# One quarter of the gate-weighted one-hots on GpSimd, and four moves around the first value tiles of an expert layer

## Chip, cores and metric

The kernel runs on one core of one Trainium2 chip. The metric is the device time of one execution in microseconds (us). The kernel before takes 2701.08 us (median of 3 runs, 2700.83 to 2701.56).

## What is computed

The reference is a network of two blocks on 256 tokens of width 1024. Nearly all the time of this case lies in two equal stages of the second block, one expert layer in each of its two layers:

```python
def peer(h, w_q, sub_keys, u_emb, v_emb):        # 8 heads, 128 keys a side, 16384 experts, top 16
    q = einsum('td,dhk->thk', x_t, w_q)
    s = einsum('thpk,hpnk->thpn', q, sub_keys)
    sv, si = lax.top_k(s, K)
    ...
    fv, fpos = lax.top_k(cand, K)
    eidx = take_along_axis(cidx, fpos, axis=-1)
    gate = softmax(fv, axis=-1)
    act = gelu(einsum('thkd,td->thk', u_emb[eidx], x_t))
    return einsum('thk,thkd->td', gate * act, v_emb[eidx])
```

## The kernel before

Nothing is gathered. The layer is computed densely: all 16384 experts are taken as 128 tiles of 128. For each tile TensorE makes the scores of 256 tokens (`u`, 128 x 1024), ScalarE applies Gelu, VectorE multiplies by a dense gate (zero where a token did not choose an expert), and TensorE adds the product with `v` (128 x 1024) onto four accumulator banks. To keep fp32 accuracy with the rounded `fp32r` type, an operand is split into a high part (a rounded copy) and a low part (the operand less its high part), and each product is three matmuls.

An expert layer `l` (0 or 1) runs in these stages, written out by hand for each engine and tied by semaphores:

1. Queries, keys and the top 16. TensorE, between other work, scores the first 14 tiles (`CHOICE_TILES`), kept in `early`.
2. The gate stage. Tokens are taken in 64 groups of four (`NG`, `GROUP`). For group `g` VectorE (`one_hots`) makes four plain one-hots in one instruction (L1517) and four gate-weighted ones in four (L1519), into one of two buffers `hot[:, g % 2]`; TensorE (`gate_products`, L714) multiplies them into one bank; ScalarE copies 114 of 128 tiles' gates from the bank to `gates` (L1010); VectorE (`gate_early`, L1529) multiplies the other 14 straight into `early`. Between two groups TensorE scores one or two of the eight slices of a further tile (`early_scores`, L689), 12 tiles over the stage (`GATE_TILES`), kept in `meanwhile` by ScalarE (L998).
3. The early values. The 26 tiles of `EARLY` already have scores, so only values are left, 12 matmuls a tile (L450). `VALUES` is their order: the 12 of `meanwhile` first, then the 14 of `early`. Per tile ScalarE makes the high part of `v` (L1019) and VectorE, in `early_expert`, makes the product with the gate (L1580, first 12 only), its high and low part (L1539, L1543), and the low part of `v` (`early_v_low`, L1543, 128x1024). Both are two tiles deep: ScalarE's high part of tile `n` waits for the values of `n - 2`. Also in this stage: the transposed input `HT` is split into parts (`split_ht_part`, from tile `SPLIT_AT` = 12 on), a diagonal for the second modulation gain is made (L1298) before tile `G2_AT` = 20 and multiplied after it (L754), and the last two tiles split the first `u` of the next stage.
4. The main loop over the other 102 tiles, scores and values, with TensorE without a pause. The change does not touch it.

SyncE issues all DMAs in one program order. `v` has three slots: the load of tile `n` waits for the low part of tile `n - 3` (`expert_v`), because the low part goes to another buffer and frees the slot. The three first `u` loads of the main loop stand together behind `v` tile 15 and wait for `early_read`, the sign that `meanwhile` has been read.

```python
for n in range(E_SLOTS, EARLY):
    fetch_v(n % E_SLOTS, v[VALUES[n]], split=base + n - E_SLOTS + 1)
    if n == GATE_TILES + E_SLOTS:
        sp.wait_ge(sem("early_read"), l + 1)
        for j in range(EARLY, EARLY + E_SLOTS):
            fetch_u(j % E_SLOTS, u[j])
```

Of the kernel before, what the change touches and what calls it, by code (L numbers as in the profile page):

```python
# [20 lines left out]
KT = D // P  # L21
T = 256
NB = T // P
# [32 lines left out]
P_SLOTS = 4  # L56
CHOICE_TILES, GATE_TILES = 14, 12
AFTER_CHOICE, AFTER_EXP = 12, 8
SPLIT_AT, G2_AT = 12, 20
EARLY = CHOICE_TILES + GATE_TILES  # L60
LATE = TILES - EARLY

# [35 lines left out]
    return [(CHOICE_TILES + n, [s % KT for s in every if s // KT == n]) for n in sorted({s // KT for s in every})]  # L98


VALUES = [*range(CHOICE_TILES, EARLY), *range(CHOICE_TILES), *range(EARLY, TILES)]


def program(nc, d, out):
    ctx = ExitStack()
    with ctx:
# [327 lines left out]
        def _(pe):  # L434
# [227 lines left out]
            def experts(l):  # L662
# [45 lines left out]
                def gate_products(g):  # L708
                    u = g % 2
                    pe.wait_ge(sem("hot"), l * NG + g + 1)  # L710
                    if g >= 2:
                        pe.wait_ge(sem("gates_kept"), l * NG + g - 1)
                    for t in range(GROUP):
                        mm = pe.matmul(ps[:, 6 + u, t * P:(t + 1) * P], hot[:, u, 1, t, :], hot[:, u, 0, t, :],  # L714
                                       start=True, stop=True)
                    mm.then_inc(sem("gates_made"), 1)
# [30 lines left out]

                base = l * TILES
                for n in range(EARLY - 1):
                    expert_values(n, base + n + 1, first=(n == 0), low=exp_uh[:, n % 2] if n < EARLY - 2 else None)  # L750
                    if n == G2_AT:
                        pe.wait_ge(sem("diag"), SPREADS[f"g2_{l}"] + 1)
                        for i in range(8):
                            mm = pe.matmul(ps[:, 6 + i // 4, i % 4 * P:(i % 4 + 1) * P], ones, g2_diag[:, i * P:(i + 1) * P], start=True, stop=True)  # L754
                        mm.then_inc(sem("g2_spread"), 1)
# [81 lines left out]
        def _(act):  # L837
# [147 lines left out]
            def experts(l):  # L985
                root(f"peer_{l}", f"mix_{l}")
                for i in range(4):
                    for j in range(2):
                        h = 2 * i + j
                        put(pq_t[:, 2 * h:2 * h + 2].rearrange("p a t -> p (a t)"), ((("pq", l, i), j), 0))  # L990
                        stored(f"pq_{l}_{h}")
                        put(sc[:, 2 * h:2 * h + 2].rearrange("p s b n -> p (s b n)"), (f"sc_{l}", h))
                        stored(f"sc_{l}_{h}")

                def keep_scores(n):
                    act.wait_ge(sem("expert_scored"), l * TILES + n + 1)
                    dst = early[:, n] if n < CHOICE_TILES else meanwhile[:, n - CHOICE_TILES]
                    act.activation(dst, ps[:, 4 + n % 2, 0:T], ACT.Gelu).then_inc(sem("early_kept"), 1)  # L998

                for n in range(AFTER_EXP):  # L1000
                    keep_scores(n)
                act.wait_ge(sem("gate_in"), l + 1)
                act.activation(chosen_h[:, 2], fin_v.rearrange("p (h b) k -> p h b k", b=NB), ACT.Exp).then_inc(sem("gate_exp"), 1)
                for n in range(AFTER_EXP, CHOICE_TILES):
                    keep_scores(n)
                act.wait_ge(sem("slots"), 2 * l + 2)

                for g in range(NG):
                    act.wait_ge(sem("gates_made"), l * NG + g + 1)
                    act.activation(gates[:, g * GROUP:(g + 1) * GROUP, :], r3(ps[:, 6 + g % 2, :], GROUP)[:, :, CHOICE_TILES:], ACT.Copy)\  # L1010
                       .then_inc(sem("gates_stored"), 1)
                    for n, steps in gate_steps(g):
                        if KT - 1 in steps:
                            keep_scores(n)
                for n in range(EARLY + 1):
                    act.wait_ge(sem(f"expert_v{n % E_SLOTS}_arrived"), 16 * (l * len(range(n % E_SLOTS, TILES, E_SLOTS)) + n // E_SLOTS + 1))
                    if n >= 2:
                        act.wait_ge(sem("expert_used"), l * (TILES + 1) + n)
                    act.activation(exp_vh[:, n % 2], exp_v[:, n % E_SLOTS], ACT.Copy).then_inc(sem("early_v_high"), 1)  # L1019
                    if n == G2_AT + 2:  # L1020
# [65 lines left out]
        def _(dve):  # L1086
# [328 lines left out]
            def experts(l):  # L1415
# [95 lines left out]
                def one_hots(g):  # L1511

                    u, at_ = g % 2, g * GROUP
                    if g >= 2:
                        dve.wait_ge(sem("gates_made"), l * NG + g - 1)
                    rows_of = slots_t[:, 0, at_:at_ + GROUP].unsqueeze(2).to_broadcast([P, GROUP, P])
                    dve.tensor_tensor(hot[:, u, 0], iota.unsqueeze(1).to_broadcast([P, GROUP, P]), rows_of, ALU.is_equal)  # L1517
                    for t in range(GROUP):
                        ins = dve.tensor_scalar(hot[:, u, 1, t, :], iota, slots_t[:, 1, at_ + t:at_ + t + 1],  # L1519
                                                slots_t[:, 2, at_ + t:at_ + t + 1], ALU.is_equal, ALU.mult)  # L1520
                    ins.then_inc(sem("hot"), 1)
# [9 lines left out]
                for g in range(NG):  # L1531
                    one_hots(g)
                    if g >= 2:
                        gate_early(g - 2)
                for g in (NG - 2, NG - 1):
                    gate_early(g)
                def high(dst, src):

                    return dve.tensor_copy(dst, src)  # L1539
# [18 lines left out]
                def early_v_low(n):  # L1558

                    v_arrived(n)  # L1560
                    dve.wait_ge(sem("early_v_high"), l * (EARLY + 1) + n + 1)
                    low(exp_uh[:, n % 2] if n < EARLY - 2 else exp_vl[:, n % E_SLOTS], exp_v[:, n % E_SLOTS], exp_vh[:, n % 2]).then_inc(sem("expert_v"), 1)

                def split_ht_part(k):

                    step(high(ht_high[:, k], HT[:, k]))
                    settle()
                    ins = low(ht_low[:, k], HT[:, k], ht_high[:, k])
                    if k == KT - 1:
                        step(ins)  # L1570
                        settle()
                        dve.sem_inc(sem("ht_split"), 1)
                    else:
                        step(ins)

                def early_expert(n):

                    dve.wait_ge(sem("expert_used"), base_v + max(n, 1))
                    if n < GATE_TILES:
                        step(dve.tensor_tensor(act_e[:, n % 2], meanwhile[:, n], gates[:, :, n], ALU.mult))  # L1580
                        x = act_e[:, n % 2]
                        settle()
                    else:
                        x = early[:, n - GATE_TILES]
                    step(high(act_h[:, n % 2], x))
                    u = n + 2
                    if u >= EARLY:
# [6 lines left out]
                    if n == GATE_TILES - 1:  # L1594
# [4 lines left out]
                    early_v_low(n)  # L1599
# [190 lines left out]
            end_rows("end2", HN)  # L1790


        @block.sync
        def _(sp):
            sp.dma_start(X.rearrange("p b n -> p (b n)"), d["x"]).then_inc(sem("x_loaded"), 16)
# [12 lines left out]
            def load_experts(l):  # L1808
# [24 lines left out]

                chunk_read(1)
                chunk_read(2)
                for n in range(P_SLOTS // 2):
                    fetch_early(n)
                chunk_read(3)
# [4 lines left out]
                for n in range(P_SLOTS, EARLY):  # L1843
                    fetch_early(n)
                for n in range(E_SLOTS, EARLY):
                    fetch_v(n % E_SLOTS, v[VALUES[n]], split=base + n - E_SLOTS + 1)
                    if n == GATE_TILES + E_SLOTS:
                        sp.wait_ge(sem("early_read"), l + 1)
                        for j in range(EARLY, EARLY + E_SLOTS):
                            fetch_u(j % E_SLOTS, u[j])  # L1850
                turns = LATE // STEP - 1
                for n in range(EARLY, EARLY + STEP):
                    if n >= EARLY + E_SLOTS:
# [164 lines left out]
```

## Time and profile before

| | us |
|---|---|
| median of 3 runs | 2701.08 (2700.83 to 2701.56) |
| the profiled execution | 2696.82, its span 2694.8 |
| TensorE matmul busy | 2483.4 (92% of the span) |
| VectorE busy | 1916.7 (71%) |
| ScalarE busy | 427.9 (16%) |
| GpSimd busy | 0.2, in four 128x1 memsets |
| gate stage, layer 0 | first group's products at 790.6, last scores end near 904.7 |
| early values, layer 0 | 908.05 to 985 |

How to read it: an engine's busy time is an average over stages with different limits. For each of the stages named above one looks at which engine runs back to back, and at what the others' idle time is put down to. Matmul records have modelled ends, so distances between starts are the safer durations. `x8` of an fp32 matmul is four matmuls of two passes each.

### The profile page before, as it was taken

The numbers are of one execution on the slowest core, as the hardware profiler recorded it, in microseconds if no ns is written. First come the engines' busy times: TensorE is split into PE (matmuls) and PEld (weight loads), VectorE is DVE, ScalarE is ACT, GpSimd is POOL, SyncE is SP. The second block draws the span as 40 slices with busy tenths as digits, with TensorE's granted clock in tenths as the row PEclk, the third lists the DMA queues.
The fourth block names the chain that finished last, engine by engine and source line by source line (L and its number), as shares of the span: only waits on it lengthen the run. The fifth ranks groups of instructions, "written<-read, shape, count | busy, mean of one in ns | idle before, by whom it ended". The sixth has DMA issues, their size and how long they took to land.

```text
span 2694.8 us, 37151 instructions
## 1 busy us (share of the span) xinstructions
PE 2483.4 (92%) x13514; PEld 2071.3 (77%) x13514; DVE 1916.7 (71%) x4362; ACT 427.9 (16%) x865; POOL 0.2 (0%) x4
## 2 busy tenths in 40 slices
PE   8987999887899999999999976689999999999997
PEld 6655787454787789999999955558777899999997
DVE  2324344453889878888888854559898888888887
ACT  2322000011123320000000023411233100000001
POOL 0000000000000000000000000000000000000000
PEclk9988999988999999999999988899999999999998
DMA  5413677733141255555555543023205455555553
GB/s 194 156 63 125 239 282 290 291 146 150 65 139 56 91 184 187 186 186 187 187 186 187 186 181 125 1 94 118 79 32 195 163 187 186 187 186 187 187 187 120
DMA packets 87211, 429.43 MB, mean 159 GB/s; under 512 B 10064, under 2 KB 10704, under 8 KB 77008
## 3 DMA queue, kind: packets, MB, share of 16 engines
q1 hardware_dynamic: 87120, 428.23, 45.0%
q8 instruction: 56, 0.92, 0.1%
q14 instruction: 35, 0.29, 0.0%
HBM read 427.14 MB, written 1.05 MB: 159 GB/s over the span
## 4 chain that ended last, share of the span: by engine, by line
PE 77%; DVE 16%; DMA 3%; ACT 2%; issue 2%; DVEq 0%; SPq 0%; ACTq 0%; PEldq 0%
PE ps L450 48%; PE ps L482 10%; PE ps L472 6%; DVE HN L1519 5%; PE ps L689 4%; DVE HN L1517 3%; PE ps L648 3%; DMA ring<-in_stream 2%; DVE arena L1271 1%; PE ps L512 1%; PE ps L530 1%; DVE HT L1151 1%; DVE arena L1529 1%; PE ps L676 1%; ACT arena L901 1%
## 5 line engine op out<-in xcount | busy, mean ns | idle before, releaser
L450 PE MATMUL ps<-ring_rounded,HN_rounded 128*128 128x512 f32 x3072 | 745.5, 393 | 11.5 <-DVE ring_rounded L1543 11.1
L450 PEld LDWEIGHTS ps<-ring_rounded,HN_rounded 128*128 128x128 f32 x3072 | 563.2, 189 | 130.5 <-issue 21.1
L450 PE MATMUL ps<-ring_rounded 128*128 128x256 f32 x3264 | 619.2, 283 | 0.0
L1543 DVE TENSOR_TENSOR ring_rounded<-ring,ring_rounded 128x1024 fp32r<-128x1024 f32 x460 | 561.9, 1222 | 16.7 <-ACT ring_rounded L1019 9.7
L450 PEld LDWEIGHTS ps<-ring_rounded 128*128 128x128 f32 x3264 | 522.3, 191 | 7.9
L450 PE MATMUL ps<-HT_rounded,ring_rounded 128*128 128x256 f32 x1632 | 461.8, 283 | 0.0
L1539 DVE CAST ring_rounded<-ring 128x1024 fp32r<-128x1024 f32 x406 | 280.5, 691 | 155.7 <-DMA ring<-in_experts_u 153.6
L482 PE MATMUL ps<-HT,ring 128*128 128x256 f32 x1472 | 335.7, 389 | 20.2 <-DVEq L1158 19.3
L482 PEld LDWEIGHTS ps<-HT,ring 128*128 128x128 f32 x1472 | 285.6, 196 | 62.4 <-DVEq L1158 21.1
L450 PEld LDWEIGHTS ps<-HT_rounded,ring_rounded 128*128 128x128 f32 x1632 | 312.5, 191 | 8.0
L1026 ACT ACTIVATE HN<-ps 128x256 f32<-128x256 f32 x204 | 78.3, 384 | 1061.6 <-PE ps L450 1061.6
L689 PE MATMUL ps<-HT,ring 128*128 128x256 f32 x832 | 201.8, 380 | 4.1 <-issue 1.5
L871 ACT ACTIVATE arena<-ps 128x512 f32<-128x512 f32 (+4 forms) x136 | 77.6, 581 | 557.2 <-PE ps L482 362.1
L689 PEld LDWEIGHTS ps<-HT,ring 128*128 128x128 f32 x832 | 148.0, 191 | 19.5 <-issue 3.1
L472 PE MATMUL ps<-ring,HT 128*128 128x512 f32 (+3 forms) x384 | 157.7, 572 | 5.1 <-DVEq L1158 5.1
L714 PEld LDWEIGHTS ps<-HN 128*128 128x128 f32 x1024 | 124.2, 191 | 47.4 <-DVE HN L1519 37.3
L714 PE MATMUL ps<-HN 128*128 128x128 f32 x1024 | 141.6, 281 | 13.8 <-DVE arena L1529 13.8
L1519 DVE TENSOR_SCALAR HN<-iota,slots_t 128x128 f32<-128x128 f32 x512 | 146.4, 375 | 0.0
L472 PEld LDWEIGHTS ps<-ring,HT 128*128 128x128 f32 x384 | 75.3, 198 | 83.1 <-issue 75.0
L1622 DVE TENSOR_TENSOR HN<-HN,arena 128x256 f32<-128x256 f32 x204 | 130.3, 639 | 10.9 <-ACT HN L1026 6.4
L1271 DVE SCALAR_TENSOR_TENSOR arena<-ring,cact,arena 128x256 f32<-128x256 f32 x336 | 135.0, 478 | 0.0
L1517 DVE TENSOR_TENSOR HN<-iota,slots_t 128x512 f32<-128x512 f32 x128 | 92.0, 719 | 9.9 <-PE ps L714 9.6
(204 smaller groups left out, 1746.7 us busy)
## 6 DMA issues: line engine op xcount, KB each, us to landing
ring<-in_stream SPq DMA_DIRECT2D x69, 2048.0 KB, 8.4
ring<-in_experts_u SPq DMA_DIRECT2D x256, 512.0 KB, 4.3
ring<-in_experts_v SPq DMA_DIRECT2D x256, 512.0 KB, 3.5
ring<-in_stream SPq DMA_DIRECT2D x2, 1024.0 KB, 7.6
arena<-in_keys SPq DMA_DIRECT2D x2, 1024.0 KB, 14.8
ring<-in_stream SPq DMA_DIRECT2D x1, 1664.0 KB, 8.3
ring<-in_stream SPq DMA_DIRECT2D x1, 1040.0 KB, 19.4
X<-in_x SPq DMA_DIRECT2D x1, 1024.0 KB, 4.9
```

What stands on the lines that cost most here:

```text
L450: mm = pe.matmul(out_, p, q, start=(first and i == 0), stop=(last and i == 2))
L472: mm = pe.matmul(t[:, 0:n], src[:, k, b * P:(b + 1) * P], w[:, k, :], start=(k == 0), stop=(k == nk - 1))
L482: mm = pe.matmul(t[:, j * T:(j + 1) * T], w[:, k, i * 256 + j * P:i * 256 + (j + 1) * P], src[:, k, :], start=(k == 0), stop=(k == KT - 1))
L648: mm = pe.matmul(down[2 * b + half], act_t[:, kt, b * P:(b + 1) * P], w[:, k, half * 512:(half + 1) * 512], start=(kt == 0), stop=(kt == F ...
L689: mm = pe.matmul(ps[:, 4 + n % 2, 0:T], pre_u[:, n % P_SLOTS, k * P:(k + 1) * P], HT[:, k, :], start=(k == 0), stop=(k == KT - 1))
L714: mm = pe.matmul(ps[:, 6 + u, t * P:(t + 1) * P], hot[:, u, 1, t, :], hot[:, u, 0, t, :], start=True, stop=True)
L1271: ins = dve.scalar_tensor_tensor(out=part, in0=wk, scalar=cact[:, k:k + 1], in1=part, op0=ALU.mult, op1=ALU.add)
L1517: dve.tensor_tensor(hot[:, u, 0], iota.unsqueeze(1).to_broadcast([P, GROUP, P]), rows_of, ALU.is_equal)
L1519: ins = dve.tensor_scalar(hot[:, u, 1, t, :], iota, slots_t[:, 1, at_ + t:at_ + t + 1], slots_t[:, 2, at_ + t:at_ + t + 1], ALU.is_equal, ...
L1539: return dve.tensor_copy(dst, src)
L1543: return dve.tensor_tensor(dst, src, h.bitcast(F32), ALU.subtract)
L1622: dve.tensor_tensor(act_e[:, j % 2], act_e[:, j % 2], g, ALU.mult).then_inc(sem("split_steps"), 1)
```

## The change

- `one_hots` makes three of the four weighted one-hots of a group; GpSimd makes the fourth, as one TENSOR_SCALAR of the same shape on the same operands, and signals `hot_last`. TensorE waits for it too. GpSimd waits, as VectorE does, until the products of group `g - 2` are made.
- `FIRST = 2`: the order of early values becomes two tiles of `early`, the 12 of `meanwhile`, the 12 other tiles of `early`.
- The first `v` tile: ScalarE makes its high part in the gate stage at group 58, VectorE its low part at group 61, in place, over the loaded tile. So the load into its slot (tile 3) waits for the values of tile 0 and no longer for its low part.
- The `u` loads stand behind `v` tiles 17, 19 and 21, one each.
- ScalarE makes the high parts of `HT` (tiles 14 to 21); VectorE keeps the low parts. The diagonal is made before tile 24 and multiplied after it.

```diff
-SPLIT_AT, G2_AT = 12, 20
+FIRST, SPLIT_AT, G2_AT = 2, 14, 24
-VALUES = [*range(CHOICE_TILES, EARLY), *range(CHOICE_TILES), *range(EARLY, TILES)]
+VALUES = [*range(FIRST), *range(CHOICE_TILES, EARLY), *range(FIRST, CHOICE_TILES), *range(EARLY, TILES)]
+def low_in_place(n):
+    return n == 0 or n >= EARLY - 2
...
                     pe.wait_ge(sem("hot"), l * NG + g + 1)
+                    pe.wait_ge(sem("hot_last"), l * NG + g + 1)
...
+                    if g == NG - 6:
+                        act.wait_ge(sem("expert_v0_arrived"), 16 * (l * len(range(0, TILES, E_SLOTS)) + 1))
+                        act.activation(exp_vh[:, 0], exp_v[:, 0], ACT.Copy).then_inc(sem("early_v_high"), 1)
-                for n in range(EARLY + 1):
+                for n in range(1, EARLY + 1):
...
+                    if SPLIT_AT <= n < SPLIT_AT + KT:
+                        k = n - SPLIT_AT
+                        act.activation(ht_high[:, k], HT[:, k], ACT.Copy).then_inc(sem("ht_high"), 1)
...
-                    for t in range(GROUP):
+                    for t in range(GROUP - 1):
                         ins = dve.tensor_scalar(hot[:, u, 1, t, :], iota, slots_t[:, 1, at_ + t:at_ + t + 1],
                                                 slots_t[:, 2, at_ + t:at_ + t + 1], ALU.is_equal, ALU.mult)
...
-                    step(high(ht_high[:, k], HT[:, k]))
-                    settle()
+                    dve.wait_ge(sem("ht_high"), l * KT + k + 1)
                     ins = low(ht_low[:, k], HT[:, k], ht_high[:, k])
...
+                    if n:
+                        early_v_low(n)
+                for g in range(NG):
+                    one_hots(g)
+                    if g >= 2:
+                        gate_early(g - 2)
+                    if g == NG - 3:
+                        early_v_low(0)
...
+        @block.gpsimd
+        def _(pool):
+            for l in range(2):
+                pool.wait_ge(sem("slots"), NB * (l + 1))
+                for g in range(NG):
+                    if g >= 2:
+                        pool.wait_ge(sem("gates_made"), l * NG + g - 1)
+                    t = g * GROUP + GROUP - 1
+                    pool.tensor_scalar(hot[:, g % 2, 1, GROUP - 1, :], iota, slots_t[:, 1, t:t + 1], slots_t[:, 2, t:t + 1],
+                                       ALU.is_equal, ALU.mult).then_inc(sem("hot_last"), 1)
...
+                U_AT = [FIRST + GATE_TILES + E_SLOTS + i for i in (0, 2, 4)]
...
+                    if low_in_place(n - E_SLOTS):
+                        fetch_v(n % E_SLOTS, v[VALUES[n]], base_v + n - E_SLOTS + 2)
+                    else:
+                        fetch_v(n % E_SLOTS, v[VALUES[n]], split=base + n - E_SLOTS + 1)
+                    if n in U_AT:
+                        j = EARLY + U_AT.index(n)
                         sp.wait_ge(sem("early_read"), l + 1)
-                        for j in range(EARLY, EARLY + E_SLOTS):
-                            fetch_u(j % E_SLOTS, u[j])
+                        fetch_u(j % E_SLOTS, u[j])
```

VectorE's queue over the end of the gate stage and the first two early tiles, layer 0, before (HN is where `hot` and the activation's parts lie, ring where `u` and `v` lie):

```order
L1529 TENSOR_TENSOR arena<-ps,arena 128x4x14 [waits gates_stored]
L1517 TENSOR_TENSOR HN<-iota,slots_t 128x512 [waits gates_made]
L1519 TENSOR_SCALAR HN<-iota,slots_t 128x128 x4
L1529 TENSOR_TENSOR arena<-ps,arena 128x4x14 [waits gates_stored] x3
L1580 TENSOR_TENSOR HN<-ring,arena 128x256 [waits gates_stored,expert_used,early_kept,dve_steps]
L1539 CAST HN_rounded<-HN 128x256 [waits dve_steps]
L1543 TENSOR_TENSOR HN_rounded<-HN,HN_rounded 128x256 [waits dve_steps]
L1543 TENSOR_TENSOR ring_rounded<-ring,ring_rounded 128x1024 [waits early_v_high,expert_v0_arrived]
```

The same place now:

```order
L1543 TENSOR_TENSOR arena<-ps,arena 128x4x14 [waits gates_stored]
L1551 TENSOR_TENSOR ring_rounded<-ring,ring_rounded 128x1024 [waits early_v_high,expert_v0_arrived]
L1531 TENSOR_TENSOR HN<-iota,slots_t 128x512 [waits gates_made]
L1533 TENSOR_SCALAR HN<-iota,slots_t 128x128 x3
L1543 TENSOR_TENSOR arena<-ps,arena 128x4x14 [waits gates_stored]
L1531 TENSOR_TENSOR HN<-iota,slots_t 128x512 [waits gates_made]
L1533 TENSOR_SCALAR HN<-iota,slots_t 128x128 x3
L1543 TENSOR_TENSOR arena<-ps,arena 128x4x14 [waits gates_stored] x3
L1547 CAST HN_rounded<-arena 128x256 [waits gates_stored,expert_used,early_kept,dve_steps]
L1551 TENSOR_TENSOR HN_rounded<-arena,HN_rounded 128x256 [waits dve_steps]
```

A group has three weighted one-hots instead of four, the low part of the first `v` tile stands two groups before the end, and only a cast and a subtraction of 128x256 are left between the gate stage and the first value matmul.

SyncE's queue over the early values, layer 0, before:

```order
L1816 DMA ring<-in_experts_u 128x1024 [waits expert_scored] x22
L1828 DMA ring<-in_experts_v 128x1024 [waits expert_v] x13
L1821 DMA ring<-in_experts_u 128x1024 [waits early_read]
L1821 DMA ring<-in_experts_u 128x1024 x2
L1828 DMA ring<-in_experts_v 128x1024 [waits expert_v] x11
```

And now:

```order
L1844 DMA ring<-in_experts_u 128x1024 [waits expert_scored] x22
L1856 DMA ring<-in_experts_v 128x1024 [waits expert_used]
L1856 DMA ring<-in_experts_v 128x1024 [waits expert_v] x14
L1849 DMA ring<-in_experts_u 128x1024 [waits early_read]
L1856 DMA ring<-in_experts_v 128x1024 [waits expert_v] x2
L1849 DMA ring<-in_experts_u 128x1024 [waits early_read]
L1856 DMA ring<-in_experts_v 128x1024 [waits expert_v] x2
L1849 DMA ring<-in_experts_u 128x1024 [waits early_read]
```

The first `v` load of the stage now waits for finished values, and the three `u` loads no longer stand in a row.

## Rows read from the trace of the kernel before

**Rows 1.** The page: span, and busy time of each engine with its share.
```profile
span 2694.8 us, 37151 instructions
PE 2483.4 (92%) x13514; PEld 2071.3 (77%) x13514; DVE 1916.7 (71%) x4362; ACT 427.9 (16%) x865; POOL 0.2 (0%) x4
```

**Rows 2.** Timeline (start us, us, engine, line, operation), VectorE, one group of gate stage 0.
```profile
841.55 0.28 DVE L1529 TENSOR_TENSOR arena<-ps,arena 128x56 f32<-128x56 f32 x1
841.71 0.72 DVE L1517 TENSOR_TENSOR HN<-iota,slots_t 128x512 f32<-128x512 f32 x1
842.31 1.14 DVE L1519 TENSOR_SCALAR HN<-iota,slots_t 128x128 f32<-128x128 f32 x4
843.34 0.29 DVE L1529 TENSOR_TENSOR arena<-ps,arena 128x56 f32<-128x56 f32 x1
```

**Rows 3.** Timeline, TensorE, the same stretch; in brackets idle time and who ended it.
```profile
840.24 1.08 PE L714 MATMUL ps<-HN 128*128 128x128 f32 x8
841.16 0.60 PE L689 MATMUL ps<-HT,ring 128*128 128x256 f32 x2
841.98 1.13 PE L714 MATMUL ps<-HN 128*128 128x128 f32 x8 [0.22 <-DVE arena L1529]
842.95 1.03 PE L689 MATMUL ps<-HT,ring 128*128 128x256 f32 x4
843.81 0.31 PE L714 MATMUL ps<-HN 128*128 128x128 f32 x1
```

**Rows 4.** Groups by form over gate stage 0 (busy us, mean ns | idle before).
```profile
L1519 DVE TENSOR_SCALAR HN<-iota,slots_t 128x128 f32<-128x128 f32 x256 | 73.2, 376 | 0.0
```

**Rows 5.** Chain of waits from the gate stage into the early values, layer 0.
```profile
905.34 0.65 DVE HN L1580
906.01 0.30 DVE HN_rounded L1539
...
906.69 1.23 DVE ring_rounded L1543
...
908.05 1.05 PE ps L450 x2
```

**Rows 6.** Windows around that passage (busy by engine, PEclk, DMA share, GB/s).
```profile
904.00:908.00 4.00, 0.70 (x4) 0.27 (x2) 2.84 (x6) 2.70 (x4) 0.00 (x0) 1.00 0.00 0
908.00:912.00 4.00, 3.95 (x10) 3.12 (x11) 2.31 (x4) 0.00 (x0) 0.00 (x0) 0.57 0.53 158
```

**Rows 7.** Timeline, TensorE, after each pause of the early values, layers 0 and 1.
```profile
956.22 11.36 PE L450 MATMUL ps<-ring_rounded,HN_rounded 128*128 128x512 f32 x48 [0.85 <-DVE ring_rounded L1543]
968.37 2.97 PE L450 MATMUL ps<-ring_rounded,HN_rounded 128*128 128x512 f32 x12 [0.80 <-DVE ring_rounded L1543]
982.28 2.98 PE L450 MATMUL ps<-ring_rounded,HN_rounded 128*128 128x512 f32 x12 [0.77 <-DVE ring_rounded L1543]
2071.65 11.39 PE L450 MATMUL ps<-ring_rounded,HN_rounded 128*128 128x512 f32 x48 [0.47 <-DVE ring_rounded L1543]
```

**Rows 8.** Timeline, TensorE elsewhere: the same 16 transposes after two idle times.
```profile
1701.44 2.05 PE L530 MATMUL ps<-arena 128*128 128x128 f32 x16 [1.52 <-ACTq L909]
243.69 3.78 PE L530 MATMUL ps<-arena 128*128 128x128 f32 x16 [2.36 <-ACTq L909]
```

**Rows 9.** Groups over the early values, layer 0, 905 to 985 us.
```profile
L1539 DVE CAST ring_rounded<-HT 128x256 fp32r<-128x256 f32 x8 | 2.3, 287 | 0.0
L1539 DVE CAST ring_rounded<-ring 128x1024 fp32r<-128x1024 f32 x2 | 1.4, 688 | 0.0
L1019 ACT ACTIVATE ring_rounded<-ring 128x1024 fp32r<-128x1024 f32 x26 | 27.5, 1060 | 48.5 <-PE ps L450 45.7 <-DMA ring<-in_experts_v 2.8
```

**Rows 10.** DMA: a window behind the u loads, and landing times of v there.
```profile
949.00:951.00 2.00, 2.00 (x10) 1.44 (x9) 1.77 (x6) 1.06 (x1) 0.00 (x0) 1.00 1.03 412
...
DMA to landing us min/median/max: 3.3/3.5/7.0
```

More of the change, by code:

```diff
@@ L749, in experts @@
                 for n in range(EARLY - 1):
-                    expert_values(n, base + n + 1, first=(n == 0), low=exp_uh[:, n % 2] if n < EARLY - 2 else None)
+                    expert_values(n, base + n + 1, first=(n == 0), low=None if low_in_place(n) else exp_uh[:, n % 2])
                     if n == G2_AT:
@@ L1529, in gate_early @@
                     dve.tensor_tensor(part, r3(ps[:, 6 + g % 2, :], GROUP)[:, :, 0:CHOICE_TILES], part, ALU.mult).then_inc(sem("gates_kept"), 1)
[L1531 to L1536, printed above, removed]
                 def high(dst, src):
@@ L1561, in early_v_low @@
                     dve.wait_ge(sem("early_v_high"), l * (EARLY + 1) + n + 1)
-                    low(exp_uh[:, n % 2] if n < EARLY - 2 else exp_vl[:, n % E_SLOTS], exp_v[:, n % E_SLOTS], exp_vh[:, n % 2]).then_inc(sem("expert_v"), 1)
+                    low(exp_vl[:, n % E_SLOTS] if low_in_place(n) else exp_uh[:, n % 2], exp_v[:, n % E_SLOTS], exp_vh[:, n % 2]).then_inc(sem("expert_v"), 1)
                 def split_ht_part(k):
-                    step(high(ht_high[:, k], HT[:, k]))
-                    settle()
+                    dve.wait_ge(sem("ht_high"), l * KT + k + 1)
                     ins = low(ht_low[:, k], HT[:, k], ht_high[:, k])
@@ L1578, in early_expert @@
                     dve.wait_ge(sem("expert_used"), base_v + max(n, 1))
-                    if n < GATE_TILES:
-                        step(dve.tensor_tensor(act_e[:, n % 2], meanwhile[:, n], gates[:, :, n], ALU.mult))
+                    if FIRST <= n < FIRST + GATE_TILES:
+                        step(dve.tensor_tensor(act_e[:, n % 2], meanwhile[:, n - FIRST], gates[:, :, n - FIRST], ALU.mult))
                         x = act_e[:, n % 2]
@@ L1583, in early_expert @@
                     else:
-                        x = early[:, n - GATE_TILES]
+                        x = early[:, VALUES[n]]
                     step(high(act_h[:, n % 2], x))
@@ L1593, in early_expert @@
                     low(act_l[:, n % 2], x, act_h[:, n % 2]).then_inc(sem("expert_gated"), 1)
-                    if n == GATE_TILES - 1:
+                    if n == FIRST + GATE_TILES - 1:
                         dve.sem_inc(sem("early_read"), 1)
@@ L1598, in early_expert @@
                         low(exp_ul[:, u % E_SLOTS], exp_u[:, u % E_SLOTS], exp_uh[:, u % 2]).then_inc(sem("expert_u"), 1)
-                    early_v_low(n)
+                    if n:
[6 more added lines that the diff above has]
+                        early_v_low(0)
+                for g in (NG - 2, NG - 1):
+                    gate_early(g)
                 settle()
@@ L1845, in load_experts @@
                 for n in range(E_SLOTS, EARLY):
-                    fetch_v(n % E_SLOTS, v[VALUES[n]], split=base + n - E_SLOTS + 1)
-                    if n == GATE_TILES + E_SLOTS:
+                    if low_in_place(n - E_SLOTS):
[4 more added lines that the diff above has]
+                        j = EARLY + U_AT.index(n)
                         sp.wait_ge(sem("early_read"), l + 1)
-                        for j in range(EARLY, EARLY + E_SLOTS):
-                            fetch_u(j % E_SLOTS, u[j])
+                        fetch_u(j % E_SLOTS, u[j])
                 turns = LATE // STEP - 1
```

## The prediction

> **What bounds it now.** I read the page first, then each of the two stages that the edits touch in the timeline, then the chain of waits between them. TensorE is busy for 92% of the span and GpSimd does nothing [rows 1], so an edit can only give back what TensorE loses, and the question is where it waits.
>
> In the gate stage the timeline of VectorE shows no gap: from one gate multiply (841.55) to the next (843.34) are 1.79 us, made of 0.16 to the plain one-hots, 0.60 to the weighted ones and 1.03 for four of them, 0.258 from start to start [rows 2]. There are 64 groups in each layer, so 64 x 1.79 = 114.6 us. TensorE in the same stretch needs, when nothing holds it, 0.92 for a group's products (840.24 to 841.16) and 0.86 for two slices of scores (842.95 to 843.81), 0.43 for one slice [rows 3]. Groups with one and with two slices alternate, so a pair costs 2 x 0.92 + 0.43 + 0.86 = 3.13, or 1.57 a group. The difference to 1.79 is the time that TensorE waits, here 0.22 for VectorE's gate multiply plus what stands before it as a modelled tail [rows 3]. So VectorE bounds this stage, by 0.22 us a group, and TensorE is close behind.
>
> Between the stages the chain shows VectorE alone: gate product 905.34, cast 906.01, low part, then 1.23 for the low part of v from 906.69, and TensorE at 908.05 [rows 5]. In the four us that follow, the granted clock of TensorE is 0.57, near the lower level of 1.2 GHz; before it was 1.00 [rows 6].
>
> In the early values TensorE runs, 11.36 us for four tiles, 2.84 a tile, with three short pauses in layer 0 (0.85, 0.80, 0.77) and in layer 1 the first of them is 0.47 [rows 7].
>
> **The change, part by part.**
>
> *One weighted one-hot less on VectorE.* VectorE's group is 1.79 - 0.258 = 1.53, below TensorE's 1.57. If GpSimd costs nothing beside it, TensorE sets the period and a group gains 0.22: 64 x 0.22 = 14.1 us a layer. The unknown is the price c that GpSimd's instruction puts on VectorE per group. No row shows GpSimd at work beyond four memsets of one column [rows 1]. The nearest row is VectorE's own instruction for the same job, 376 ns long, and its slot of 258 ns [rows 4, 2]. Lower end: c = 0, since GpSimd takes work off VectorE and could at best leave it alone. Upper end: VectorE stands still for a whole such instruction, c = 0.376. What I take is between, from this: each group has one moment, the 0.16 of the gate multiply, in which VectorE reads the bank, and not two operands of SBUF or a constant row. If GpSimd's work takes a slot of 0.258 and 0.16 of it falls there, about 0.10 is lost. The period is then 1.53 + 0.10 = 1.63 and a group gains 0.16, or 64 x 0.16 = 10.2 us a layer.
>
> The Trainium skill speaks against this edit (SBUF — State Buffer, section on SBUF's two separate sides): VectorE and GpSimd share a port pair that is an exclusive lock, taken for a whole instruction, by a VectorE instruction with two SBUF inputs or in a two-port mode. That VectorE has such a mode the trace agrees with: a cast of 128x1024 takes 688 ns and one of 128x256 takes 287, half a nanosecond an element [rows 9]. By that rule nearly every instruction of the group would collide; no row here shows it, and the sum would be the rival of the lock below instead of the forecast.
>
> *GpSimd as a new thing to wait for.* It is released with VectorE, when the products of g - 2 are made, and its result is wanted when TensorE comes to g. Between them TensorE has one slice pair, one product group and one slice, 0.86 + 0.92 + 0.43 = 2.2 us. An instruction of up to about 1.6 us, four times VectorE's own 376 ns [rows 4], is hidden. I take nothing. Behind the waiting TensorE nothing else is queued that could go ahead.
>
> *The low part of v tile 0 in the stage.* It adds 1.2 us to VectorE two groups before the end [rows 5]. With a slack near 0 it costs 1.2 us a layer. ScalarE's 1.06 for the high part [rows 9] lies in idle time of ScalarE, which is busy 16% of the span [rows 1], and can hold one gate multiply back once; nothing more.
>
> *The passage.* The product (0.67, 905.34 to 906.01) and the low part of v with its wait (908.05 - 906.34 less 0.43 for the low part of the activation, which stays and starts at 906.34) go [rows 5]. What stays is 0.33 + 0.43 + 0.14, so TensorE starts near 906.24, 1.8 us earlier. Its idle time before falls from 3.3 (4.00 less 0.70 busy [rows 6]) to about 1.5. That matters a second time. Sixteen transposes took 2.05 us after 1.52 idle and 3.78 after 2.36 [rows 8]; so the short pause should leave the clock at 2.4 GHz. In window 908 to 912 it was at 0.57 for four us [rows 6], which is 4 x 0.43 = 1.7 us of work. Passage: -1.8 - 1.7 = -3.5 us a layer.
>
> *Tile 3 loaded later.* Its load used to go out before the first matmul; now it waits for the values of tile 0, 2.84 us into the stage. It lands 3.5 later [rows 10], then 1.06 of ScalarE [rows 9] and 1.23 of VectorE [rows 5] and some 0.4 of handing over: 9.1. TensorE wants it after three tiles, at 8.5. A new pause of 0.6 us a layer. (With a slow clock at the start it would be hidden; then 1.7 is lost instead.)
>
> *The u loads apart.* The first pause, 0.85 and 0.47, comes from three u loads ahead of a v load: v landed after 7.0 us, where 3.5 is usual, with the DMA engines full at 412 GB/s [rows 10]. Spread over five tiles (14 us) they add 1.5 MB to 2.6 MB, some 300 GB/s, under that. Both pauses go: -1.3 us in all.
>
> *HT's high parts on ScalarE.* VectorE loses eight casts of 287 ns; ScalarE gets eight, each shorter than its 1.06 for four times the width, and has 48.5 us idle in the stage [rows 9]. TensorE waits for neither in these tiles once the load is in time. Nothing.
>
> *The diagonal from tile 20 to 24.* The pause of 0.80 at tile 20 goes. But tile 24 already has a pause of 0.77, because VectorE also splits a u there [rows 7]. Its low part of v for tile 23 ends 0.1 + 1.06 + 0.1 + 1.2 = 2.45 after the values of 21; with 1.2 for the diagonal that is 3.7, 0.8 past the end of the values of 22, where tile 24's work wants to start. The pause there becomes 0.77 + 0.8. Nothing in all; from -1 to +1.
>
> **The sum**, in one layer: gate stage -10.2 + 1.2 = -9.0; passage -3.5; tile 3 +0.6. Twice that is -23.8. The pauses behind the u loads -1.3. Together -25 us, on a profiled execution of 2696.8, that is 2672. It lies 4.3 us under the median of the runs, so I state it against the median: 2701.1 - 25 = **2676 us**.
>
> **The rivals.** Fixed parts without the one-hots are -3.5, +0.6 and +1.2 in each layer and -1.3, about -5 us.
>
> *TensorE sets the pace.* GpSimd costs VectorE nothing, 128 x 0.22 = -28; the low part of v is then mostly hidden too. 2676 becomes 2670. For it: GpSimd's work is small and released at the same moment as VectorE's. Against: both read the same two tensors at the same time.
>
> *An even trade.* GpSimd costs VectorE just the slot it takes off, c = 0.258. Only the fixed -5 is left: 2696.
>
> *The lock; slower.* VectorE is stopped for the whole of GpSimd's instruction, at least its own 376 ns for that work [rows 4]. The group becomes 1.53 + 0.376 = 1.91, +0.12 x 128 = +15 us, less 5: 2711. Every further 0.1 us is 12.8 us more. It decides from c = 0.30 on (0.258 + 5/128), and beyond 0.34 it is slower by more than can be read as noise. For it: VectorE has hardly a gap in a group [rows 2]. Against: nothing in this trace. This is where the rule of the port pair leads.
>
> *GpSimd late; slower too.* If its instruction takes more than 1.79 us from release to release, GpSimd is the new bound and the period is its time. At 2.0 us that is +27 - 5, 2723. It needs five times VectorE's 376 ns.
>
> **Chances.** What a measurement of this kernel can tell from no change is about 0.2%, 5.4 us. Forecast 0.39, TensorE's pace 0.21, even trade 0.19 (half of it just over the bound, half within), lock 0.16, GpSimd late 0.05. Faster 0.39 + 0.21 + 0.09 = 0.69, same 0.10, slower 0.21. The range reaches from TensorE's pace with tile 3 hidden (2670 less 1 or 2) to the lock at its lowest price, 2711, and leaves out the long lock and the late GpSimd: 2668 to 2712. If the one-hots go well the time lies in 2668 to 2684.
>
> **What would show it.** Right: the distance of two gate multiplies on VectorE near 1.63, VectorE's weighted one-hots still near 376 ns, TensorE's wait in front of the products at nearly nothing in groups with two slices, the first value matmul less than 1.6 us after the last scores and granted clock 1.00 behind it, no pause at tile 16, a pause near 0.6 at tile 3 and one near 1.6 at tile 24. Wrong: one-hots of 500 ns and more or gaps between them while GpSimd is busy (the lock), or TensorE waiting for GpSimd (late). The forecast is wrong if the gate stage is not shorter by at least 5 us a layer.

## The result, and the profile after

The changed kernel takes 2667.62 us (median of 4 runs, 2664.36 to 2668.93), the kernel before, on the same chip, 2700.95 us (2699.69 to 2701.56). The ratio is 0.9876 (95% interval 0.9864 to 0.9888): 33.3 us faster, where 25 were forecast. The time lies 0.4 us under the low end of the range.

| | before | after |
|---|---|---|
| profiled execution, its span | 2696.82, 2694.8 | 2666.75, 2665.0 |
| TensorE matmul busy | 2483.4 | 2471.7 |
| VectorE busy | 1916.7 | 1883.7 |
| GpSimd busy | 0.2 | 177.4 |
| last group's products start, layer 0 | 902.71 | 890.44 |
| first value matmul, layers 0 and 1 | 908.05, 2023.86 | 893.89, 1995.83 |

The profiled executions are 30.1 us apart, the medians 33.3.

The timeline of VectorE and GpSimd, two groups of gate stage 0 of the changed kernel, answers to [rows 2]:

```profile
835.72 0.69 DVE L1531 TENSOR_TENSOR HN<-iota,slots_t 128x512 f32<-128x512 f32 x1
835.79 2.74 POOL L1817 TENSOR_SCALAR HN<-iota,slots_t 128x128 f32<-128x128 f32 x2 [0.41 <-PE ps L722]
836.33 0.92 DVE L1533 TENSOR_SCALAR HN<-iota,slots_t 128x128 f32<-128x128 f32 x3
837.10 0.25 DVE L1543 TENSOR_TENSOR arena<-ps,arena 128x56 f32<-128x56 f32 x1
837.26 0.69 DVE L1531 TENSOR_TENSOR HN<-iota,slots_t 128x512 f32<-128x512 f32 x1
...
838.69 0.24 DVE L1543 TENSOR_TENSOR arena<-ps,arena 128x56 f32<-128x56 f32 x1
838.85 0.69 DVE L1531 TENSOR_TENSOR HN<-iota,slots_t 128x512 f32<-128x512 f32 x1
```

A plain one-hot starts at 835.72, 837.26 and 838.85: 1.54 and 1.59 us a group instead of 1.79. VectorE's instructions are no longer than before (0.69 and 0.72 for the plain ones), though GpSimd is inside an instruction for 1.37 us of each group.

TensorE beside it, answering to [rows 3]:

```profile
837.76 1.05 PE L722 MATMUL ps<-HN 128*128 128x128 f32 x8
838.65 0.60 PE L696 MATMUL ps<-HT,ring 128*128 128x256 f32 x2
839.08 1.13 PE L722 MATMUL ps<-HN 128*128 128x128 f32 x8
840.05 1.03 PE L696 MATMUL ps<-HT,ring 128*128 128x256 f32 x4
840.91 1.05 PE L722 MATMUL ps<-HN 128*128 128x128 f32 x8
```

No idle time stands in brackets any more, in either kind of group. From 837.76 to 840.91 a pair takes 3.15 us, where 3.13 had been worked out as TensorE's own need. TensorE sets the pace of this stage now. GpSimd is not far behind: its two records fill 2.74 of the 3.15 us.

The groups by form over gate stage 0 show the new work on GpSimd, and against [rows 4] that VectorE's one-hot kept its length:

```profile
L1817 POOL TENSOR_SCALAR HN<-iota,slots_t 128x128 f32<-128x128 f32 x64 | 88.7, 1388 | 800.8 <-DVEq L1523 783.2 <-PE ps L722 17.4
L722 PE MATMUL ps<-HN 128*128 128x128 f32 x512 | 69.4, 278 | 0.7 <-DVE arena L1543 0.7
...
L1533 DVE TENSOR_SCALAR HN<-iota,slots_t 128x128 f32<-128x128 f32 x192 | 58.4, 373 | 0.0
```

TensorE's pauses from the end of that stage on, layer 0, then the two in the early values of layer 1. They answer to [rows 7]:

```profile
886.21 1.11 PE L722 MATMUL ps<-HN 128*128 128x128 f32 x8
...
888.85 1.13 PE L722 MATMUL ps<-HN 128*128 128x128 f32 x8 [0.67 <-DVE arena L1543]
...
890.44 1.13 PE L722 MATMUL ps<-HN 128*128 128x128 f32 x8
...
893.89 8.77 PE L457 MATMUL ps<-ring_rounded,HN_rounded 128*128 128x512 f32 x36 [1.45 <-DVE HN_rounded L1551]
903.09 59.77 PE L457 MATMUL ps<-ring_rounded,HN_rounded 128*128 128x512 f32 x252 [0.43 <-DVE ring_rounded L1551]
964.42 2.98 PE L457 MATMUL ps<-ring_rounded,HN_rounded 128*128 128x512 f32 x12 [1.56 <-DVE ring_rounded L1551]
...
2004.86 59.86 PE L457 MATMUL ps<-ring_rounded,HN_rounded 128*128 128x512 f32 x252 [0.27 <-DVE ring_rounded L1551]
2066.25 2.96 PE L457 MATMUL ps<-ring_rounded,HN_rounded 128*128 128x512 f32 x12 [1.53 <-DVE ring_rounded L1551]
```

The two groups beside the low part of v tile 0 take 4.23 us (886.21 to 890.44) instead of 3.15, so it costs 1.1 us, of which 0.67 stands in brackets; the passage is 1.45 instead of 3.35; tile 3 has the new pause (0.43, 0.27); tile 16 has none; tile 24 has 1.56. Behind the passage the clock stays up, where [rows 6] had 0.57:

```profile
892.00:896.00 4.00, 2.55 (x12) 1.81 (x11) 2.74 (x6) 1.49 (x3) 0.00 (x0) 1.00 0.00 0
896.00:900.00 4.00, 3.96 (x18) 2.98 (x18) 2.85 (x5) 1.06 (x1) 0.00 (x0) 1.00 0.51 155
```

### The profile page after: what moved, and what is told of

It reads as the page before. It is cut to its first block, busy times and chain, and to the rows that moved or that the text cites. A ratio compares the mean times of both kernels' runs of the same rounds, so it can differ in the third digit from the quotient of the medians.

```text
span 2665.0 us, 37157 instructions
## 1 busy us (share of the span) xinstructions
PE 2471.7 (93%) x13514; PEld 2075.6 (78%) x13514; DVE 1883.7 (71%) x4218; ACT 432.8 (16%) x881; POOL 177.4 (7%) x132
## 4 chain that ended last, share of the span: by engine, by line
PE 80%; DVE 14%; ACT 2%; DMA 2%; issue 1%; DVEq 0%; SPq 0%; ACTq 0%; PEldq 0%
PE ps L457 50%; PE ps L489 11%; PE ps L479 7%; DVE HN L1533 4%; PE ps L696 4%; DVE HN L1531 3%; PE ps L655 3%; DMA ring<-in_stream 1%; PE ps L519 1%; DVE arena L1285 1%; PE ps L537 1%; DVE HT L1165 1%; PE ps L683 1%; ACT arena L909 1%; DVE arena L1543 1%
## 5 line engine op out<-in xcount | busy, mean ns | idle before, releaser
L1817 POOL TENSOR_SCALAR HN<-iota,slots_t 128x128 f32<-128x128 f32 x128 | 177.2, 1387 | 1814.2 <-DVEq L1523 1778.9
L1533 DVE TENSOR_SCALAR HN<-iota,slots_t 128x128 f32<-128x128 f32 x384 | 116.6, 373 | 0.0
```

Of the source, the lines that this page charges most:

```text
L1817: pool.tensor_scalar(hot[:, g % 2, 1, GROUP - 1, :], iota, slots_t[:, 1, t:t + 1], slots_t[:, 2, t:t + 1], ALU.is_equal, ALU.mult).then_in ...
```

## Experiments

### The one-hot alone, and the rest alone

The kernel before with nothing but the one-hot moved:

```diff
+                    pe.wait_ge(sem("hot_last"), l * NG + g + 1)
-                    for t in range(GROUP):
+                    for t in range(GROUP - 1):
                         ins = dve.tensor_scalar(hot[:, u, 1, t, :],
...
+        @block.gpsimd
...
```

> The kernel before with the one-hot moved to GpSimd and nothing else. Theory (TensorE's own pace is all that is left, GpSimd's instruction costs VectorE nothing): the gate stage gains what the trace of the change shows, (1.78 - 1.575) x 64 = 13 us a layer, so -26 us in all, about 2675; the 3.35 us passage, its slow clock and the pauses of 0.85, 0.80 and 0.77 stay. Rival (the price c of 0.10 us that the prediction took is real and the other edits gave the rest): -20 us, about 2681.

Measured: 2674.0 us against 2699.91, ratio 0.9904 (0.9889 to 0.9919), -25.9 us. This is the theory's -26. Its passage is still 3.35 us long:

```profile
895.40 47.46 PE L450 MATMUL ps<-ring_rounded,HN_rounded 128*128 128x512 f32 x192 [3.35 <-DVE ring_rounded L1544]
943.19 11.36 PE L450 MATMUL ps<-ring_rounded,HN_rounded 128*128 128x512 f32 x48 [0.33 <-DVE ring_rounded L1544]
955.36 2.98 PE L450 MATMUL ps<-ring_rounded,HN_rounded 128*128 128x512 f32 x12 [0.82 <-DVE ring_rounded L1544]
```

The changed kernel with all four one-hots back on VectorE:

```diff
-                    pe.wait_ge(sem("hot_last"), l * NG + g + 1)
-                    for t in range(GROUP - 1):
+                    for t in range(GROUP):
-        @block.gpsimd
...
```

> The changed kernel with all four weighted one-hots back on VectorE and GpSimd idle. Theory: the passage stays short (-1.9 and about -1.7 of clock), the u loads' pauses are gone, tile 3 has its new pause; but the low part of v tile 0 costs its full 1.2 us a layer, as VectorE has no slack in the gate stage. Twice (-1.9 - 1.7 + 0.4 + 1.2) - 1.3 = -5 us, about 2696. Rival (the four other edits are worth more than I summed, and the one-hots less): -10 us or more, 2691 or less.

Measured: 2693.01 us, ratio 0.9973 (0.9964 to 0.9981), -6.9 us, between the two expectations and nearer the theory's -5. The two halves add up: -25.9 - 6.9 = -32.8, the whole -33.3. So they do not need each other, and four fifths of the gain are the one-hots.

### Does GpSimd's instruction cost VectorE anything?

In the kernel before, VectorE bounds the gate stage without slack, so there a price shows at full size. GpSimd makes a fifth one-hot per group that nobody uses:

```diff
+        spare = ring[:, 10 * D:10 * D + P]
+                    pool.tensor_scalar(spare, iota, slots_t[:, 1, t:t + 1], slots_t[:, 2, t:t + 1],
+                                       ALU.is_equal, ALU.mult).then_inc(sem("dup"), 1)
```

> The kernel before, VectorE still making all four weighted one-hots, and GpSimd making a fifth per group that nobody uses, of the same form, into spare room. VectorE bounds the gate stage here without slack (1.787 us a group), so a price that GpSimd puts on it shows at full size. Theory (no price): 1.787 stays, no change of the time within 2 us. Rival (port lock, GpSimd's 1.38 us or a part of it stops VectorE): from 0.1 us a group, +13 us, to 1.38 us, +177 us; with one lock of 0.376 it would be +48 us.

Measured: 2698.13 us, ratio 0.9995 (0.9984 to 1.0006). The upper end of the interval leaves 1.6 us, 0.013 a group; a price of 0.10 would have been 12.8 us. The groups by form, 800 to 890 us:

```profile
L1805 POOL TENSOR_SCALAR ring<-iota,slots_t 128x128 f32<-128x128 f32 x52 | 78.0, 1500 | 14.9 <-PE ps L715 14.9
L1520 DVE TENSOR_SCALAR HN<-iota,slots_t 128x128 f32<-128x128 f32 x203 | 57.7, 381 | 0.0
```

The price c is zero: VectorE's one-hots take 381 ns beside a busy GpSimd and 376 without [rows 4]. GpSimd is the one that gives way: its instruction takes 1500 ns here, 1388 in the changed kernel, where VectorE makes one one-hot less, and 0.79 us where VectorE is idle, as the next run shows. The prediction's c of 0.10 us and the lock's 0.376 both fall for this instruction.

### Two of four one-hots on GpSimd

```diff
-                    for t in range(GROUP - 1):
+                    for t in range(GROUP - 2):
...
+                    for i in (GROUP - 2, GROUP - 1):
+                        t = g * GROUP + i
+                        ins = pool.tensor_scalar(hot[:, g % 2, 1, i, :], iota, ...
```

> The changed kernel with two of four weighted one-hots on GpSimd. Theory: GpSimd's instructions cost it 1.37 us each from start to start and it becomes the bound: 2.74 us a group against 1.575, +75 us a layer, about 2667 + 150 = 2817. VectorE's instructions keep their length (weighted about 0.35, plain about 0.69). Rival (GpSimd's 1.38 is mostly waiting for VectorE's port): with VectorE less busy the instruction gets clearly shorter than 1.38, and the time is well under 2817.

Measured: 2722.46 us, ratio 1.0082 (1.0062 to 1.0101): slower, but by far less than 150 us. GpSimd and VectorE in its gate stage:

```profile
835.16 10.08 POOL L1818 TENSOR_SCALAR HN<-iota,slots_t 128x128 f32<-128x128 f32 x10
...
836.44 0.79 POOL L1818 TENSOR_SCALAR HN<-iota,slots_t 128x128 f32<-128x128 f32 x1
837.22 0.79 POOL L1818 TENSOR_SCALAR HN<-iota,slots_t 128x128 f32<-128x128 f32 x1
837.72 0.69 DVE L1531 TENSOR_TENSOR HN<-iota,slots_t 128x512 f32<-128x512 f32 x1 [1.09 <-PE ps L722]
837.99 1.18 POOL L1818 TENSOR_SCALAR HN<-iota,slots_t 128x128 f32<-128x128 f32 x1
839.16 1.30 POOL L1818 TENSOR_SCALAR HN<-iota,slots_t 128x128 f32<-128x128 f32 x1
...
839.27 0.69 DVE L1531 TENSOR_TENSOR HN<-iota,slots_t 128x512 f32<-128x512 f32 x1 [0.17 <-PE ps L722]
```

Ten instructions fill 10.08 us without a gap, 1.0 us each and 2.0 a group. From 1.575 to 2.0 a group over 128 groups is +55 us, on 2667.6 that is 2722: as measured. So GpSimd was the bound here, and the rival "GpSimd late" is real at this load.

The 1.0 is a mean of unlike ones. The two instructions that fall mostly into VectorE's idle 1.09 us take 0.79 each, the two after them, beside VectorE's one-hots, 1.18 and 1.30. That is the rival that the expectation named: a good part of the 1.38 us goes to VectorE's work beside it, and with VectorE less busy the instruction is shorter.

### Which instructions of GpSimd do hold VectorE

The kernel before, and an unused product of two 128x1024 blocks once every four groups:

```diff
+                    pool.tensor_tensor(spare, X[:, 0, :], X[:, 1, :], ALU.mult).then_inc(sem("dup"), 1)
```

> The kernel before, and GpSimd multiplies two 128x1024 blocks of SBUF into spare room once every four groups of the gate stage; nobody uses the product. Theory (VectorE is never held by GpSimd): VectorE's groups stay at 1.787 us while GpSimd works, the time stays within 2 us of before. Rival (an instruction of GpSimd that is long enough holds the shared port): VectorE shows a gap or long one-hots of 1 us or more beside each of the 16 products of a layer, +32 us or more in all.

Measured: 2788.59 us, ratio 1.0329 (1.03 to 1.0358), +87 us. My theory that GpSimd never holds VectorE falls. The timeline around one product:

```profile
842.86 3.27 DVE L1520 TENSOR_SCALAR HN<-iota,slots_t 128x128 f32<-128x128 f32 x4
843.70 2.34 POOL L1804 TENSOR_TENSOR ring<-X 128x1024 f32<-128x1024 f32 x1 [6.97 <-PE ps L715]
846.04 0.24 DVE L1530 TENSOR_TENSOR arena<-ps,arena 128x56 f32<-128x56 f32 x1
846.19 0.68 DVE L1518 TENSOR_TENSOR HN<-iota,slots_t 128x512 f32<-128x512 f32 x1
846.40 1.34 PEld L715 LDWEIGHTS ps<-HN 128*128 128x128 f32 x8 [2.75 <-DVE HN L1520]
```

Four one-hots of VectorE take 3.27 us instead of 1.11. VectorE's next instruction starts when GpSimd's 2.34 us end, at 846.04. VectorE stood still for 2.16 us, and TensorE waited for it 2.75. The same kernel shows TensorE's clock down for a while behind such stops (mean granted 0.90 over 783 to 906 us, where the kernel before has 1.00), which adds to the 2.2 us each: 87 us are 2.7 for each of 32 products.

Two more runs separate the kind of instruction from its width. The first makes an unused product of two 128x128 blocks in every group:

```diff
+                    pool.tensor_tensor(spare, X[:, 0, 0:P], X[:, 1, 0:P], ALU.mult)
```

> The kernel before and, in every group, an unused product of two 128x128 blocks on GpSimd. Separates width from kind. If two SBUF inputs on GpSimd are what holds VectorE, each of 128 products costs it the time in which it reads, 128 of 1024 columns of the 2.2 us seen: 0.27 us, +35 us in all. If it is the width or the length of the record alone, nothing, as with the one-hot.

The second makes an unused one-hot, 128x1024, once every four groups:

```diff
+                    pool.tensor_scalar(spare, X[:, 0, :], slots_t[:, 1, g:g + 1], slots_t[:, 2, g:g + 1],
+                                       ALU.is_equal, ALU.mult)
```

> The kernel before and, every four groups, an unused weighted one-hot of 128x1024 on GpSimd: the one-hot's form with one tensor input, at eight times its width. If one tensor input never holds VectorE: no change within 2 us. If every instruction of GpSimd holds it while it streams, and the narrow one only streams too short a time to be seen: VectorE shows one long instruction of a microsecond or more beside each, +40 us or more.

Measured: 2732.98 us, ratio 1.0133 (1.0112 to 1.0153), +34.5 us, for the narrow product; 2726.78 us, ratio 1.011 (1.0089 to 1.013), +28 us, for the wide one-hot. The narrow product:

```profile
837.57 1.38 DVE L1520 TENSOR_SCALAR HN<-iota,slots_t 128x128 f32<-128x128 f32 x4
838.41 0.46 POOL L1804 TENSOR_TENSOR ring<-X 128x128 f32<-128x128 f32 x1 [1.60 <-PE ps L715]
838.87 0.24 DVE L1530 TENSOR_TENSOR arena<-ps,arena 128x56 f32<-128x56 f32 x1
```

The wide one-hot:

```profile
840.39 3.82 POOL L1804 TENSOR_SCALAR ring<-X,slots_t 128x1024 f32<-128x1024 f32 x1 [4.09 <-PE ps L715]
840.56 0.25 DVE L1530 TENSOR_TENSOR arena<-ps,arena 128x56 f32<-128x56 f32 x1
840.72 1.44 DVE L1518 TENSOR_TENSOR HN<-iota,slots_t 128x512 f32<-128x512 f32 x1
842.08 1.10 DVE L1520 TENSOR_SCALAR HN<-iota,slots_t 128x128 f32<-128x128 f32 x4
```

| on GpSimd | its record beside a busy VectorE, us | VectorE held by it, us |
|---|---|---|
| one-hot, 128x128 (one tensor input) | 1.38 to 1.50 | 0 |
| one-hot, 128x1024 | 3.82 | 1.44 - 0.68 = 0.76 |
| product, 128x128 (two tensor inputs) | 0.46 | 1.38 - 1.11 = 0.27 |
| product, 128x1024 | 2.34 | 3.27 - 1.11 = 2.16 |

The length of a record says nothing of the price. The shortest, 0.46 us, would have cost VectorE 0.27 us in each group, as much as the one-hot moved off it (0.258); the one-hot in use is three times as long and free. Products cost 2.1 ns a column at both widths. The wide one-hot holds VectorE's plain one-hots once (1.44), but not the weighted ones (1.10) that still run inside its record; 32 times 0.76 are 24 of the 28 us. That is 0.74 ns a column, but the narrow one costs not the 0.09 us that this rate gives; why it slips through is open. Nor is the form alone shown to decide: the wide one-hot and both products read `X`, the narrow one-hot reads `iota`, and no run changes that by itself.

### Built on the change

The changed kernel, with both parts of v tile 0 made at the start of the gate stage, where VectorE waits 5.2 us for the first products, in room that HT's high parts take only from tile 14 on:

```diff
+        v0_high, v0_low = ring_r[:, 10 * D:11 * D], ring_r[:, 11 * D:12 * D]
-    return n == 0 or n >= EARLY - 2
+    return n >= EARLY - 2
-                    if g == NG - 3:
+                    if g == 1:
                         early_v_low(0)
```

The changed kernel itself ran beside it.

> The changed kernel itself, on the same chip as the two variants that build on it. Expected: the ratio of 0.9876 again, within 0.9864 to 0.9888.

> The changed kernel, but both parts of v tile 0 are made before the second pair of groups, in room that HT's high parts take only from tile 14 on: VectorE is idle for 5.2 us there. Theory: the pause of 0.67 us three groups before the end of the gate stage goes, and v tile 3 can be loaded before the first value matmul, so its pause of 0.43 and 0.27 goes: -2.0 us against the changed kernel. Rival (tile 3's pause comes from ScalarE's chain and not from the late load): only -1.3.

Measured: 2668.16 us, ratio 0.9881 (0.9862 to 0.9901) for the change again, and 2669.13 us, 0.9883 (0.9862 to 0.9905) for the variant: no gain. But its pauses changed:

```profile
797.20 1.13 PE L723 MATMUL ps<-HN 128*128 128x128 f32 x8 [1.35 <-DVE arena L1545]
896.42 68.28 PE L458 MATMUL ps<-ring_rounded,HN_rounded 128*128 128x512 f32 x288 [1.45 <-DVE HN_rounded L1553]
966.27 3.00 PE L458 MATMUL ps<-ring_rounded,HN_rounded 128*128 128x512 f32 x12 [1.56 <-DVE ring_rounded L1553]
```

288 matmuls run in one piece, so tile 3's pause did come from the late load. A new pause of 1.35 stands at the third group. VectorE's row there names its cause:

```profile
792.80 0.38 ACT L1009 ACTIVATE arena<-ps 128x256 f32<-128x256 f32 x1 [3.07 <-PE ps L697]
793.09 1.05 ACT L1019 ACTIVATE ring_rounded<-ring 128x1024 fp32r<-128x1024 f32 x1
...
793.76 0.79 POOL L1820 TENSOR_SCALAR HN<-iota,slots_t 128x128 f32<-128x128 f32 x1 [5.38 <-PE ps L723]
...
794.24 1.23 DVE L1553 TENSOR_TENSOR ring_rounded<-ring,ring_rounded 128x1024 fp32r<-128x1024 f32 x1 [5.78 <-ACT ring_rounded L1019]
```

ScalarE comes to the high part only after the scores of tile 13 (792.80), in program order, and VectorE spends its idle time waiting for it. GpSimd's one-hot takes 0.79 us there too, next to the idle VectorE. The diagonal one tile earlier:

```diff
-FIRST, SPLIT_AT, G2_AT = 2, 14, 24
+FIRST, SPLIT_AT, G2_AT = 2, 14, 23
```

> As the run before, and the diagonal is made before tile 23 instead of 24. Theory: tile 24's pause falls from 1.56 to 0.77, since VectorE has only the activation's and v's parts at tile 23, and at tile 23 at most 0.2 is left: -0.6 us a layer more, -3.2 against the changed kernel in all. Rival (the late start is passed on from tile to tile): the pause only moves, no gain over the run before.

Measured: 2665.6 us, ratio 0.988 (0.9858 to 0.9902). Tile 24's pause is gone in both layers; by the time alone no difference can be told. With ScalarE's high part put before the scores of tile 12:

```diff
-                for n in range(AFTER_EXP, CHOICE_TILES):
+                for n in range(AFTER_EXP, AFTER_CHOICE):
                     keep_scores(n)
+                act.activation(v0_high, exp_v[:, 0], ACT.Copy).then_inc(sem("early_v_high"), 1)
+                for n in range(AFTER_CHOICE, CHOICE_TILES):
+                    keep_scores(n)
```

> As the run with both parts of v tile 0 early and the diagonal before tile 23, but ScalarE makes the high part before it keeps the scores of tile 12, so that VectorE has both in its idle 5.2 us. Theory: the pause of 1.35 us at the third group was VectorE waiting for that high part behind ScalarE's two late copies of scores; it goes in both layers, -2.7 us against that run, -3.5 to -5 us against the change, about 2663. Rival (the third group waits for something else): 1.35 stays.

> The same kernel as the run with v tile 0 before tile 12, timed again, since its ratio of 0.9864 (0.9848 to 0.9881) overlaps that of the change. Theory: its pauses are gone for good, so the ratio is again 0.986 to 0.987, 1 to 2 thousandths under the change's 0.9876 and 0.9881. Rival: it was luck of a run, and the ratio is 0.988 or more.

Measured: 2660.71 us, ratio 0.9864 (0.9848 to 0.9881), and again 2660.33 us, 0.9857 (0.9837 to 0.9877). All pauses of TensorE in layer 0, from the gate stage to the main loop:

```profile
786.73 7.14 PE L697 MATMUL ps<-HT,ring 128*128 128x256 f32 x32 [1.56 <-issue]
895.84 68.57 PE L458 MATMUL ps<-ring_rounded,HN_rounded 128*128 128x512 f32 x288 [1.45 <-DVE HN_rounded L1555]
```

Only the passage is left. Both medians lie 7 us under the change's 2667.6 and 2668.2, and the ratios 1 to 2 thousandths under its 0.9876 and 0.9881. Each interval overlaps the change's, so the gain of 3 to 6 us is likely and not proven; it is the best version of this study.

## Why the prediction was wrong

**The bound, right.** VectorE held the gate stage at 1.79 us a group and TensorE's own need was put at 1.57. After the change the pair took 3.15 us, 1.575 a group.

**The price c, wrong: the step that failed.** The prediction took c = 0.10 us of VectorE's time per group, from the thought that GpSimd's work is as long as a slot of VectorE's and must find room between its instructions. Measured c is 0: the two do get in each other's way, but it is GpSimd that waits, 1.38 to 1.50 us for work that takes 0.79 beside an idle VectorE. The period of 1.63 was 1.575. That is the rival "TensorE sets the pace", given 0.21. By the starts of the last products the stage gained 902.71 - 890.44 = 12.3 us, with the low part of v tile 0 in it, where the forecast had 9.0: 3.3 us a layer, 6.6 in all.

**The low part of v tile 0, right.** Priced at 1.2 us, it cost 1.1 (4.23 less 3.15). VectorE's own pace is 1.54 against 1.575, so it has hardly any slack to hide it. With all four one-hots on VectorE it cost 1.1 too. The rival's "mostly hidden" was wrong.

**The end of the range, added wrongly.** The rival at TensorE's pace was given as 2670, but its own terms, -28 and about -5, make -33, or 2668. In the -5 stand 2.4 us for the low part, which the same sentence calls mostly hidden: without them it is -35, or 2666, and less the 1 or 2 us of tile 3 the range should have begun near 2665. With the low part at the measured 1.1 twice, the same terms give -28 - 7 + 2 = -33, the 33.3 that came. So the time fell outside the range, by 0.4 us, through this sum.

**The passage, right.** 1.45 us idle against about 1.5 forecast, and granted clock 1.00 behind it. The first 36 value matmuls took 8.77 us, 5.8 for 24; before, the first 24 took 7.33 (908.05 to 915.39 in the chain of waits), with ten of them in the window at 0.57 [rows 6]. That is 1.5 us, where 1.7 was forecast.

**Tile 3, right in kind.** A pause of 0.43 and 0.27 where 0.6 was forecast, and the variant that frees the load removed it.

**The u loads, right.** No pause at tile 16 in either layer. With the one-hot alone the pause was still there, at 0.33. **HT's high parts and the diagonal, right**: nothing from the first, 1.56 at tile 24 against a forecast of 0.77 + 0.8.

**GpSimd as a thing to wait for, right.** It was taken to hide up to about 1.6 us, and its record is 1.39, 3.7 times VectorE's. It is closer than that reads: of the 1.575 of a group only 0.2 is left, and beside the low part of v tile 0 one of its instructions takes 2.49.

**What the terms do not explain.** In the profiled executions layer 0 gained 15.9 us and layer 1 16.0. Of these 31.9 the gate stages are 24.6, and the rest, 7.3, is what was forecast for the other parts (7.1). But the two spans are only 29.8 apart: 2.1 was given back between the layers. 1.3 of it lies in one row, the 32 matmuls that open the mixing stage of layer 1: 15.70 us before, 17.04 after. The granted clock tells the two apart: over the first 7.8 us it was 0.56 and then 0.99 before, 0.50 and then 0.70 after, which is about 1.4 us of work at the full clock. The change again had 17.07, at 0.50 and 0.68; the one-hot alone and the rest alone 15.70. Why the clock came back later no run shows. The medians are 33.3 apart, and the 3.5 us between that and the spans have no row either.

## What to carry to other kernels

Put GpSimd's price where it can be seen: run the instruction for nothing beside an engine that is the bound, and read that engine's rows. Its record's length says neither what it costs the neighbour (0.46 us cost 0.27, 1.4 us cost nothing) nor how fast it can go (0.79 us beside an idle VectorE, 1.4 beside a busy one). Of the forms tried here, the narrow one-hot was free beside a busy VectorE and the products were not. A pause in brackets is not a cost either: 0.67 stood there, and the distance of starts said 1.1. And when a rival is summed, add its terms again under its own conditions: here that would have put the end of the range some 3 us lower.

## What the runs showed of the hardware

- A one-hot of 128x128 on GpSimd takes 0.79 us beside an idle VectorE, 1.38 beside one that makes three weighted one-hots a group, and 1.50 beside one that makes four. It costs VectorE nothing (376 and 381 ns).
- A product of two SBUF blocks on GpSimd stops VectorE: 0.27 us of its 0.46 at 128 columns, 2.16 at 1024, nearly its whole 2.34. The Trainium skill (SBUF — State Buffer, SBUF: two separate sides) says that the shared port pair is held for a whole instruction. For the wide product this agrees; for the narrow one it is 0.27 of 0.46, and for the one-hots it does not, 0.76 of 3.82 us and none of 1.38.
- After an idle time of 1.45 us TensorE kept its 2.4 GHz (granted 1.00); after 3.35 it had been at 0.57 for four us, between the levels of 1.2 and 2.4 GHz and near the lower.
